# A gather of expert rows cut into blocks of one head instead of two

## The reference, cut to what matters

```python
def block(xb):                                   # 256 tokens
    q = (xb @ w_q).reshape(256, 8, 2, 128)       # 8 heads, two half queries
    s = einsum('thcd,hcnd->thcn', q, sub_keys)   # scores against 128 keys per half
    top_s, top_i = top_k(s, 16)
    cand = top_s[:, :, 0, :, None] + top_s[:, :, 1, None, :]
    best_s, best_c = top_k(cand.reshape(256, 8, 256), 16)
    e = (i1 * 128 + i2).reshape(256, 8 * 16)     # 128 experts of 16384 per token
    gate = softmax(best_s)                       # per head
    u = expert_u[e]                              # gathered rows, 1024 wide
    act = gelu(einsum('td,ted->te', xb, u))
    return einsum('te,ted->td', gate * act, expert_v[e])
```

## Time and profile before

| | |
|---|---|
| median of 3 runs | 1722.4 us (1721.68 to 1722.91) |
| the profiled execution, its own time | 1721.23 us |
| span of that execution | 1719.5 us |
| granted TensorE clock, mean | 0.921 |
| first fetch issued at | 960.74 us |
| last of the 512 fetches done on POOL at | 1703.54 us |

### The profile page before, as it was taken

One profiled execution on the slowest core, in us unless ns is written; L12 is line 12 of the kernel. 1 busy time (PEld: TensorE's weight loads), 2 busy tenths in 40 slices (PEclk: granted clock), 3 DMA queues, 4 the chain that ended last, 5 costly groups with the idle time before them and its releaser, 6 DMA issues.

```text
span 1719.5 us, 25059 instructions
## 1 busy us (share of the span) xinstructions
PE 1418.2 (82%) x9296; PEld 1075.0 (63%) x9296; DVE 1081.0 (63%) x2107; ACT 561.8 (33%) x1047; POOL 531.5 (31%) x620
## 2 busy tenths in 40 slices
PE   8999999986999997999988946867767649767675
PEld 7889999976999996878788832322222213222222
DVE  5556774486776445887765885676556457657444
ACT  5554653357564334423242113111111112111111
POOL 8100000010000000000000475666666666667573
PEclk9999999998999998999999977978888878999898
DMA  7344555543464543221243798999999999999996
GB/s 239 122 147 124 179 188 172 171 132 126 149 193 148 189 154 98 95 79 52 75 148 122 278 395 300 376 352 364 366 362 364 359 380 356 380 373 387 348 387 260
DMA packets 206242, 407.91 MB, mean 237 GB/s; under 512 B 10626, under 2 KB 136876, under 8 KB 206140
## 3 DMA queue, kind: packets, MB, share of 16 engines
q0 software_dynamic: 74096, 269.52, 40.9%
q1 hardware_dynamic: 131884, 136.54, 24.9%
q10 hardware_dynamic: 160, 0.53, 0.1%
HBM read 405.49 MB, written 1.05 MB: 236 GB/s over the span
## 4 chain that ended last, share of the span: by engine, by line
PE 50%; issue 17%; POOL 13%; DVE 9%; another core or an unknown queue 6%; ACT 3%; DMA 2%; POOLq 0%; DVEq 0%; SPq 0%; ACTq 0%
PE banks L2039 11%; PE banks L2041 11%; PE banks L2040 11%; POOL arena L869 5%; POOL wring L869 4%; PE banks L2217 4%; PE banks L2458 3%; POOL h_raw L869 2%; PE banks L2314 1%; PE banks L2208 1%; POOL xT L869 1%; POOL sq L869 1%; PE banks L2024 1%; DVE arena L1894 1%
## 5 line engine op out<-in xcount | busy, mean ns | idle before, releaser
L1337 DVE TENSOR_TENSOR w_a_low<-wring,w_a_high 128x1024 fp32r<-128x1024 f32 x184 | 225.2, 1226 | 130.3 <-ACT w_a_high L910 128.3
L869 POOL DMA_INDIRECT arena<-in_expert_u_dram,eidx x99 | 93.2, 942 | 674.6 <-DVEq L1874 610.6
L910 ACT ACTIVATE w_a_high<-wring 128x1024 fp32r<-128x1024 f32 x184 | 193.3, 1053 | 147.1 <-PE banks L2041 145.3
L2493 PE MATMUL banks<-arena 128*128 128x512 f32 x340 | 171.7, 652 | 72.2 <-issue 53.6
L1280 ACT ACTIVATE arena<-ident,arena 128x128 f32<-128x128 f32 x238 | 84.2, 395 | 442.6 <-remote 232.3
L2039 PE MATMUL banks<-h_high,w_a_high 128*128 128x256 f32 x768 | 219.3, 286 | 7.9 <-DVE h_low L1345 7.3
L2040 PE MATMUL banks<-h_low,w_a_high 128*128 128x256 f32 x768 | 216.6, 282 | 0.0
L2041 PE MATMUL banks<-h_high,w_a_low 128*128 128x256 f32 x768 | 216.5, 282 | 0.0
L2493 PE MATMUL banks<-wring,arena 128*128 128x512 f32 x308 | 152.9, 642 | 48.9 <-issue 37.0
L2493 PEld LDWEIGHTS banks<-arena 128*128 128x128 f32 x340 | 67.7, 207 | 174.9 <-issue 154.9
L2039 PEld LDWEIGHTS banks<-h_high,w_a_high 128*128 128x128 f32 x768 | 145.6, 190 | 9.7 <-issue 7.6
(11 more groups left out here) (395 smaller groups left out, 2886.6 us busy)
## 6 DMA issues: line engine op xcount, KB each, us to landing
wring<-in_mlp_w_dram SPq DMA_DIRECT2D x64, 1024.0 KB, 5.4
wring<-in_w_in_dram SPq DMA_DIRECT2D x19, 1024.0 KB, 5.2
wring<-in_sb_w_qkv_dram SPq DMA_DIRECT2D x12, 1024.0 KB, 5.1
wring<-in_rg_w_in_dram SPq DMA_DIRECT2D x8, 1024.0 KB, 5.9
wring<-in_w_q_dram SPq DMA_DIRECT2D x8, 1024.0 KB, 5.2
wring<-in_sb_w_o_dram SPq DMA_DIRECT2D x4, 1024.0 KB, 6.2
wring<-in_rg_w_o_dram SPq DMA_DIRECT2D x4, 1024.0 KB, 5.2
wring<-in_w_o_dram SPq DMA_DIRECT2D x4, 1024.0 KB, 7.7
```

Source lines behind the costliest of these rows:

```text
L869: g.indirect_dma_start(out=grow(j), out_offset=None, in_=(expert_u, expert_v)[which][0], in_offset=bass.IndirectOffsetOnAxis(ap=eidx[:, tt ...
L910: a.activation(unit(n, 0), raw_unit(n), ACT.Copy).then_inc(w_high, 1)
L1337: v.tensor_tensor(unit(n, 1), raw_unit(n), unit(n, 0).bitcast(F32), ALU.subtract).then_inc(w_split, 1)
L2493: last = mm(y_banks[tt][half][:, :], diag[:, n % DIAGS, :], grow(j)[:, 512 * half:512 * (half + 1)], start=False, stop=True, skip_group_ch ...
```

## The change

A block becomes one head: 16 blocks of 16 experts, 8 per tile (`PER`). `LAG` stays 2, so fetches 0 to 17 are U rows, and the last 16 are V rows. Softmax share, Exp and Gelu are made for 16 columns at a time, 16 times. `choose` works on one head: parts 2, 3 and 4 for block b + 1 come after dots 1, 3 and 5 of block b, and parts 0 and 1 for block b + 2 after dots 10 and 13. Heads 0 and 1 are chosen ahead of the loop as before. In block 0 there is no choosing; in block 1 the five parts for block 2 come after dots 2, 3, 4, 5 and 6. The last block has 6 rows on PE and 10 on DVE, where it had 14 and 18.

```diff
-BLOCKS = 8
-BSEL = 32
+BLOCKS = 16
+PER = BLOCKS // 2
+BSEL = 16
@@ POOL
-                    if b < BLOCKS and (r == 0 or b == 0 and r == TOPK):
-                        pool.wait_ge(eidx_ready, b + 2 if b or r else 1)
+                    if b < BLOCKS and r == 0:
+                        pool.wait_ge(eidx_ready, b + 1)
@@ ACT
-                act.wait_ge(gsel_ready, b + 2)
+                act.wait_ge(gsel_ready, b + 1)
...
-                    if b == 4 and r in (0, 12):
-                        finish(0, r // 12)
+                    if b == PER + 1 and r in (0, 8):
+                        finish(0, r // 8)
@@ DVE
-            def choose(b, part, heads=(0, 1)):
+            def choose(b, part):
 
-                tt, h0, nh = b // 4, 2 * (b % 4) + heads[0], len(heads)
+                tt, h0, nh = b // PER, b % PER, 1
...
-            for h in range(2):
+            for b in range(2):
                 for part in range(5):
-                    choose(0, part, (h,))
+                    choose(b, part)
             for b in range(BLOCKS + 1):
...
-                    picks = (2, 7, 12, 17, 22) if b else (9, 10, 11, 12, 13)
-                    if b < BLOCKS - 1 and r in picks:
-                        choose(b + 1, picks.index(r))
-                    if b == 5 and r in (2, 6, 24):
-                        finish(0, (2, 6, 24).index(r))
+                    if 1 <= b < BLOCKS - 2 and r in (10, 13):
+                        choose(b + 2, (10, 13).index(r))
+                    if b == 1 and r in (2, 3):
+                        choose(2, r - 2)
+                    picks = (1, 3, 5) if b > 1 else (4, 5, 6)
+                    if 1 <= b < BLOCKS - 1 and r in picks:
+                        choose(b + 1, 2 + picks.index(r))
+                    if b == PER + 2 and r in (2, 6, 12):
+                        finish(0, (2, 6, 12).index(r))
                     if b > 0 and r == LAG - 1:
                         share(b - 1)
```

More of the change, by code:

```diff
@@ L856, in fetch @@
             def fetch(b, which, r):
-                tt, c = b // 4, BSEL * (b % 4) + r
+                tt, c = b // PER, BSEL * (b % PER) + r
                 j, before = gather_row(b, which, r)
@@ L1258, in exponents @@
             def exponents(b):
-                act.wait_ge(gsel_ready, b + 2)
-                g3 = gsel[:, b // 4, BSEL * (b % 4):BSEL * (b % 4 + 1)]
-                a.activation(g3, g3, ACT.Exp, scale=rtok[:, 2 + b // 4:3 + b // 4]).then_inc(gsel_exp, 1)
+                act.wait_ge(gsel_ready, b + 1)
+                g3 = gsel[:, b // PER, BSEL * (b % PER):BSEL * (b % PER + 1)]
+                a.activation(g3, g3, ACT.Exp, scale=rtok[:, 2 + b // PER:3 + b // PER]).then_inc(gsel_exp, 1)
             exponents(0)
@@ L1266, in _ @@
             for b in range(BLOCKS):
-                tt, c0 = b // 4, BSEL * (b % 4)
+                tt, c0 = b // PER, BSEL * (b % PER)
                 act.wait_ge(dots_ready, b + 1)
@@ L1843, in choose @@
                 if part == 0:
-                    wait_out(dve, f"sc{tt}_{h0}")
+                    wait_out(dve, f"sc{tt}_{h0 if b < 2 else h0 - h0 % 2}")
                     first8(topv[:, hc], topi[:, hc], (sc, scores1)[tt][:, hc], rest)
@@ L1899, in share @@
             def share(b):
-                tt, c0 = b // 4, BSEL * (b % 4)
+                tt, c0 = b // PER, BSEL * (b % PER)
                 g3 = gsel[:, tt, c0:c0 + BSEL].rearrange("p (h s) -> p h s", s=TOPK)
                 dve.wait_ge(gsel_exp, b + 1)
-                link(v.tensor_reduce(psm[:, 0:2], g3, AX.X, ALU.add))
-                link(v.reciprocal(psm[:, 0:2], psm[:, 0:2]))
-                link(v.tensor_tensor(g3, g3, psm[:, 0:2].unsqueeze(2).broadcast_to([P, 2, TOPK]), ALU.mult))
+                link(v.tensor_reduce(psm[:, 0:1], g3, AX.X, ALU.add))
+                link(v.reciprocal(psm[:, 0:1], psm[:, 0:1]))
+                link(v.tensor_tensor(g3, g3, psm[:, 0:1].unsqueeze(2).broadcast_to([P, 1, TOPK]), ALU.mult))
                 dve.wait_ge(gelu_ready, b + 1)
@@ L1929, in finish @@
                 if part == 0:
-                    b, r = [at for at in PE_ROWS if at[0] == 4 * tt + 3][-1]
+                    b, r = [at for at in PE_ROWS if at[0] == PER * (tt + 1) - 1][-1]
                     j, before = gather_row(b, 1, r)
@@ L1952, in _ @@
             dve.wait_ge(io_ready, 1)
-            for h in range(2):
+            for b in range(2):
                 for part in range(5):
-                    choose(0, part, (h,))
+                    choose(b, part)
             for b in range(BLOCKS + 1):
-                if b < BLOCKS and b % 4 == 0:
-                    wait_group(dve, f"xn{b // 4}_1")
+                if b < BLOCKS and b % PER == 0:
+                    wait_group(dve, f"xn{b // PER}_1")
                 for r in range(BSEL + LAG):
@@ L2478, in _ @@
             for b in range(BLOCKS):
-                tt = b // 4
-                if b % 4 == 0:
+                tt = b // PER
+                if b % PER == 0:
                     wait_out(pe, f"hn{tt}_0", f"hn{tt}_1", "sc0_6", *[f"sc1_{2 * m}" for m in range(4)])
```

## The result

The changed kernel takes **1753.47 us**, median of four runs (1734.62 to 1762.18); the kernel before takes 1722.04 (1721.54 to 1722.91). The ratio is 1.0158, with a 95% interval of 1.0121 to 1.0196: slower, by 31.4 us at the medians. The forecast was 1736, with a range up to 1757. The four runs are 1762.18, 1754.40, 1734.62 and 1752.55. The longest of them counts as a slow run, so the ratio leaves it out and is lower than the 1.8% between the medians.

A forecast was written before the change was run, and what follows sets the result against it. It took a loop as the bound: full DMA, ACT late with V rows, POOL stopping in 14 episodes (84.7 us). 1721.2 + 8.4 (start) + 5 (steady) + 0 (tail) = 1734.6; the runs' median being 1.2 higher, 1736 us, range 1710 to 1757.

The forecast's parts named there:

- Rival 2: Start of the gather: ACT's stall is not shortened, so +26 there and +5 after, 1753 us; chance 0.15.
- Rival 4: Added small DVE operations lengthen POOL's fetch instructions, 18 us on top, 1753 us; chance 0.05.
- Start of the gather: First fetches up to fetch 64: POOL stops twice, and fetch 64 comes at 1070.9 against 1062.5, 8.4 us later.
- the second stop: Start of the gather: POOL stands before fetch 48 until about 1051, waiting for head 2's row numbers.
- Steady part: From fetch 64 on: added ACT and DVE work hides, transitions between blocks do not; +5 us, bounds 0 and +10.
- U rows at fault, which would make DVE the one that is late: Sign in the changed kernel's profile that would prove the forecast wrong; it expected V rows at fault in each episode.
- DVE is not the one that is late, and splitting its work helps only if it becomes one: Steady part: POOL's stops come from V rows waiting for diagonals on ACT, never from U rows.
- hidden; if it were not, it would be the whole 29: Steady part: about 29 us more DVE work costs nothing, as DVE is idle for 231 us there.
- The added transitions: Steady part: every episode, not every second, now holds a block transition; all 14 at 6.7 us is +10, taken as +5.
- Tail: End of the gather: the last four V rows stay on DVE and end the chain; 0 us.
- Rival 3: Whole gather: DMA bound, the late start is made good by fewer stops and the time stays 1722 us; chance 0.12.
- Rival 1: Steady part: shorter pieces keep slots moving, episodes shrink to 4.5 us, 1709 us; faster if their mean is under 5.4; chance 0.22.

## Why the prediction was right, and where it was not

The direction was right, and the time lies inside the range, 17.5 us above the forecast. That it lies inside is in part luck: it is outside the forecast's own case (1723 to 1745) and where rivals 2 and 4 had their 1753, and neither of these happened. The start was right in its course; the steady part was right in sign only, and for another reason than the one given.

- **Start of the gather.** Forecast: fetch 64 at 1071, Gelu 0 at 1034, the second stop until 1051. Measured: 1068.25, 1030.34 and 1048.21. The two stops came as described, the second behind the row numbers of head 2. The price, +8.4, was +5.8 by the clock and +3.3 counted from the first fetch. Two errors offset each other. POOL ended at 1023.9, not at 1018. And the 10.1 us of ACT's list, right as a length (from the copy at 1016.38 to the end of Gelu at 1030.65, less 4.11 idle, are 10.2), had been put behind the draining of DMA, while ACT did most of it ahead of that: from the copy at 1027.06 only 3.6 were left. Rival 2 (ACT not freed early) is out.
- **Steady part.** Forecast: +5, 14 episodes at 6.4 us, V rows behind ACT in each. Measured: +35.9 in the profiled run, 15 episodes, nine of them at 9.6 us, eight of these with a U row behind DVE and then the row numbers. The sign "U rows at fault, which would make DVE the one that is late" is what came. The step that failed is "DVE is not the one that is late, and splitting its work helps only if it becomes one", and with it "hidden; if it were not, it would be the whole 29". DVE's own busy time grew by 12 us, not 29; the price lies not in its amount but in where it is due. The 231 us of idleness in this part looked like room, but much of it is crawl: a bunch with 11.5 us of work takes 31. With one stop at the start removed the same work costs 8 us, and a pause of 64 us costs 37 even in the kernel before.
- **The added transitions.** They were the reason given for the +5. The kernel without the second stop has them all and is 8 us over the kernel before on the same chip, so they cost about that at most. The added table loads (29 in all, at 1283 ns) came as forecast.
- **The term that was missing: the phase.** The prediction had the 32 fetches of the cycle and the 32 of the new block, but did not lay one beside the other. A crawl that recurs after about 32 fetches met a kernel with 64 fetches a block before, and meets one with 32 after. That they meet is measured: nine long bunches in a row, against 2 near 28 us among 13 without the second stop, each from one profile. That the equal periods are what holds them together, and the stop what brings them together, is inferred; no run has varied the period. It would also explain the spread of 1735 to 1762: the fewer blocks are held, the shorter the run; but only the longest was profiled.
- **Tail.** Forecast 0, measured −0.8.
- **Rival 3** (DMA bound, 1722) fails here, and is close to what happens on chip 9: +0.15%. **Rival 1** (faster) needed a mean episode under 5.4 us; they came at 7.9.
- **Rival 4** (small operations hold POOL up): the mean of the 512 fetches is 945 ns against 942, and two of them are over 1.1 us against five before. Its 18 us are not there. The one long fetch, 1.86 us at 1504.31, runs beside an operation of `finish` over 128x1024 on DVE, which the kernel before has too. The prediction named the Trainium skill, "SBUF — State Buffer", section "SBUF: two separate sides", for this rival; a POOL that is locked out by the added copies would show as longer fetches, and no run here shows that.

## What to carry to other kernels

When an engine's busy time leaves room, ask in which stretches it has it: here 231 idle us on DVE were no room for short dependent work that came due in the full ones. When a change alters the period of a pipeline that stalls periodically, lay the new period beside that of the stalls, and look at what comes due at the same point of each; by these runs, putting off one early stop can matter more than all the work that was added. Before you read a long idle time as an engine's own slowness, look for the last input it needed. And measure on more than one chip before a cost of 2% is put down to the code.

## What was not expected of the hardware

- **Two kinds of chips.** The kernel before takes 1719 to 1722 us on chip 7 (and in the first measurement), and 1651.2 to 1651.8 on three others; the change cost 1.6% in the first measurement and 0.15% on chip 9. On the first kind the gather alternates between some 411 and 307 GB/s, on chip 9 it stays at 409. Each of these chips was visited at one time only, so whether the difference belongs to the chip or to the time is open.
- **The crawl.** On the first kind DVE has 1.6 to 2.4 us of idleness ahead of operations of 0.2 to 0.3 us, and ACT made one diagonal after 9.48 us though PE had freed its slot. From 1068 to 1560 us the idle times of DVE whose end the trace leaves unnamed add up to some 138 us in the changed kernel of the first measurement and 139 in the kernel before on chip 7: the change did not add to the crawl; it brought work that is due into it. In the changed kernel on chip 9, with DMA at the same 409 GB/s all the time, there are none. What sets it off stays open.
- **A queue of five is too short.** With five fetches of 524 KB under way the rate is 384 GB/s instead of 409, and the kernel is 38 us longer.
- **Two increments in front of a fetch are hidden**: the interval stays at 1.24 us.
